# A mask moved from VectorE into TensorE's score sums, and a norm's squares moved to ScalarE, in a two-block transformer kernel

## The reference, cut to what matters

```
z = q . k * 64 ** -0.5
before = s < t
log_1m = where(before, log_sigmoid(-z), 0)
log_rem = reverse_cumsum(log_1m) - log_1m
a = where(before, exp(log_sigmoid(z) + log_rem), 0)
o = a @ v
```

```
a = p[:, :, 0] - lam_full * p[:, :, 1]
o = a @ v
o = rms_norm(o, subln_g) * (1.0 - lam_init)
```

## Time and profile before

| | |
|---|---|
| median of 3 runs | 3639.57 us (3628.84 to 3641.31) |
| span of the profiled execution, first to last instruction | 3623.5 us |
| the profiled execution's own time | not listed apart from the runs |
| TensorE, VectorE, ScalarE busy | 84%, 67%, 35% of the span |
| stick attention | 2152.7 to 2216.1 us |
| differential attention | 2732.4 to 2769.8 us |
| its norm and transposes | 2770.0 to 2785.0 us |
| mean granted clock of TensorE | 0.895 of 2.4 GHz |

### The profile page before, as it was taken

The page is one execution under the profiler, slowest core; times in us unless marked ns, Lnnn a source line. Parts: engine busy times, 40 slices in busy tenths (PEclk is TensorE's granted clock), DMA queues, the critical chain, the costliest instruction groups (busy, mean ns, idle before and its releaser), DMA issues. The chain is left out here.

```text
span 3623.5 us, 52173 instructions
## 1 busy us (share of the span) xinstructions
PE 3031.8 (84%) x21162; PEld 2543.3 (70%) x21162; DVE 2419.6 (67%) x4307; ACT 1260.3 (35%) x2037; POOL 516.0 (14%) x305
## 2 busy tenths in 40 slices
PE   7977765665556699888999988999997999997899
PEld 4856752222211399878989886998986898987798
DVE  3677748888898777555768726777735775556554
ACT  1043211111111234364343445344344434344633
POOL 1010025555455200000000050000041000000000
PEclk9987777777777899979999997999997999998999
DMA  8932228999999786414848531867651774553153
GB/s 340 384 138 95 84 88 364 394 398 395 386 409 404 309 353 232 170 46 188 329 187 351 206 141 47 350 226 308 266 193 61 281 276 171 184 188 113 51 196 126
DMA packets 123103, 854.18 MB, mean 236 GB/s; under 512 B 17301, under 2 KB 18581, under 8 KB 21013
## 3 DMA queue, kind: packets, MB, share of 16 engines
q1 hardware_dynamic: 85748, 582.69, 42.0%
q0 software_dynamic: 36864, 268.45, 18.2%
q10 hardware_dynamic: 288, 0.26, 0.0%
HBM read 850.24 MB, written 1.11 MB: 235 GB/s over the span
## 5 line engine op out<-in xcount | busy, mean ns | idle before, releaser
L193 DVE TENSOR_TENSOR w_lo<-w_ring,w_hi 128x2048 fp32r<-128x2048 f32 x300 | 686.4, 2290 | 508.1 <-ACT w_hi L188 506.2
L268 PE MATMUL ps<-h_hi,w_hi 128*128 128x256 f32 x3328 | 954.9, 287 | 49.8 <-DVE h_lo L459 26.2
L269 PE MATMUL ps<-h_lo,w_hi 128*128 128x256 f32 x3328 | 950.9, 286 | 0.0
L270 PE MATMUL ps<-h_hi,w_lo 128*128 128x256 f32 x3328 | 950.4, 286 | 0.0
L188 ACT ACTIVATE w_hi<-w_ring 128x2048 fp32r<-128x2048 f32 x330 | 629.7, 1913 | 654.7 <-PE ps L270 634.9
L268 PEld LDWEIGHTS ps<-h_hi,w_hi 128*128 128x128 f32 x3328 | 643.8, 193 | 59.6 <-DVE h_lo L459 29.0
L269 PEld LDWEIGHTS ps<-h_lo,w_hi 128*128 128x128 f32 x3328 | 644.0, 194 | 3.2
L270 PEld LDWEIGHTS ps<-h_hi,w_lo 128*128 128x128 f32 x3328 | 643.7, 193 | 0.0
L2955 PE MATMUL ps<-expert_rows,expert_diag 128*128 128x512 f32 x412 | 289.3, 843 | 228.0 <-ACT expert_diag L2996 228.0
L193 POOL TENSOR_TENSOR w_lo<-w_ring,w_hi 128x2048 fp32r<-128x2048 f32 x30 | 138.2, 4622 | 2251.7 <-ACT w_hi L188 2251.7
L2955 PEld LDWEIGHTS ps<-expert_rows,expert_diag 128*128 128x128 f32 x412 | 92.6, 247 | 416.9 <-ACT expert_diag L2996 339.8
(11 more groups left out here) (461 smaller groups left out, 4215.7 us busy)
## 6 DMA issues: line engine op xcount, KB each, us to landing
w_ring<-in_w_stream SPq DMA_DIRECT2D x376, 1024.0 KB, 4.8
a_ring<-in_a_stream SPq DMA_DIRECT2D x108, 1024.0 KB, 7.2
a_ring<-in_t_stream SPq DMA_DIRECT2D x36, 1024.0 KB, 10.0
a_ring<-in_m_stream SPq DMA_DIRECT2D x8, 1024.0 KB, 7.1
alibi<-in_alibi SPq DMA_DIRECT2D x3, 2048.0 KB, 9.0
cond_row<-in_cond_row SPq DMA_DIRECT2D x8, 512.0 KB, 3.8
expert_rows<-in_experts,expert_idx POOLq DMA_INDIRECT x206, 11.8
gates<-mod_rows SPq DMA_DIRECT2D x3, 1024.0 KB, 5.8
```

Source lines behind the costliest of these rows:

```text
L193: pool.tensor_tensor(self.w_halves(n)[1], self.w_item(n), self.w_halves(n)[0], ALU.subtract).then_inc(self.lo_made, 1)
L268: pe.matmul(out, stationary[0], moving[0], start=start, stop=False)
L269: pe.matmul(out, stationary[0], moving[1], start=False, stop=False)
L270: return pe.matmul(out, stationary[1], moving[0], start=False, stop=stop)
```

## The change

The table `before` and its product are dropped. `after` is added by TensorE: for each half one matmul of the identity with `after` is accumulated onto the scores' diagonal block, so that everything made from S sees the mask. The wait for the table stands in front of TensorE's first scores in place of VectorE's first logits. Differential attention takes all heads of token tile 0 first and those of tile 1 after them. ScalarE squares each output from PSUM, with the sum over a head's 128 values, in front of its copy. The norm block then has a scale, a root, a reciprocal and one multiply by tile left; the gain is a column of 128 that the last copies on ScalarE use as their scale, since the transposes have put the head's values on partitions; the transposes go by token tile and wait for their own tile alone. A load of the root's table is asked for at the head of ScalarE's queue in that block.

```diff
@@ attention, vector
-            if mixer.tables:
+            if mixer.tables and not mixer.masked_scores:
                 dve.wait_ge(tables.sem, tables.at(16 * mixer.tables))
@@ Diff
+        self.ss = core.sb(ctx, "diff_ss", [P, TT, DIFF_HEADS])
+        self.sq = core.sb(ctx, "sq", [P, TT, D])
+    def at(self, p):
+        t, h = divmod(p, DIFF_HEADS)
+        return h, t, slice(t * P, (t + 1) * P), causal(t)
     def out(self, act, p):
         h, t, _, _ = self.at(p)
+        act.activation(self.sq[:, t, h * P:(h + 1) * P], self.out_bank(p), ACT.Square, accum_out=self.ss[:, t, h:h + 1])
         return act.activation(self.o[:, t, h * P:(h + 1) * P], self.out_bank(p), ACT.Copy)
@@ Stick
-    tables = 2
+    masked_scores = True
+    tables = 1
     def score(self, pe, p):
         pair, _, tok, n = self.at(p)
-        return [pe.matmul(self.bank(p, half)[:, 0:n], self.qT[part, pair, tok], self.kT[part, pair, 0:n],
-                          start=True, stop=True) for half, part in enumerate(HALVES)]
+        if p == 0:
+            loaded = self.core.semaphore_of("tables_in")
+            pe.wait_ge(loaded.sem, loaded.at(16 * self.tables))
+        for half, part in enumerate(HALVES):
+            pe.matmul(self.bank(p, half)[:, 0:n], self.qT[part, pair, tok], self.kT[part, pair, 0:n],
+                      start=True, stop=False)
+        return [pe.matmul(self.bank(p, half)[:, tok], self.core.ident[:], self.after[:], start=False, stop=True)
+                for half in range(2)]
     def logits(self, dve, p, L, mx):
-        steps.done(dve, dve.tensor_tensor(soft[:, :, tok], soft[:, :, tok], spread(self.before[:], 2), ALU.mult))
...
-        last = dve.tensor_tensor(L[:, :, 0:n], S, scan, ALU.subtract)
-        steps.done(dve, last)
-        return dve.tensor_tensor(L[:, :, tok], L[:, :, tok], spread(self.after[:], 2), ALU.add)
+        return dve.tensor_tensor(L[:, :, 0:n], S, scan, ALU.subtract)
@@ stick_stage
-        projections(core, 12, units, tables=[(n.before[:], "before"), (n.after[:], "after")], led=LEAD)
+        projections(core, 12, units, tables=[(n.after[:], "after")], led=LEAD)
@@ diff_stage
-        g = core.sb(ctx, "subln_g", [P, P])
+        g = core.sb(ctx, "subln_g", [P, 1])
-                            (g[:], core.io["subln_g"].partition_broadcast(P), consts)])
+                            (g[:], core.io["subln_g"], consts)])
@@ its vector
-                core.dve_steps.done(dve, dve.tensor_tensor(sq[:], n.o[:], n.o[:], ALU.mult))
-                core.dve_steps.done(dve, dve.tensor_reduce(st[:, 0], sq4, AX.X, ALU.add))
-                dve.tensor_scalar(st[:, 0], st[:, 0], 1.0 / P, EPS, ALU.mult, ALU.add).then_inc(ss.sem, 1)
+                dve.tensor_scalar(n.ss[:], n.ss[:], 1.0 / P, EPS, ALU.mult, ALU.add).then_inc(ss.sem, 1)
+                dve.tensor_scalar(g[:], g[:], n.keep, None, ALU.mult).then_inc(gained.sem, 1)
                 dve.wait_ge(roots.sem, roots.at(1))
-                core.dve_steps.done(dve, dve.reciprocal(st[:, 1], st[:, 0]))
+                core.dve_steps.done(dve, dve.reciprocal(n.ss[:], n.ss[:]))
                 for t in range(TT):
-                    core.dve_steps.done(dve, dve.tensor_tensor(sq4[:, t], o4[:, t], wide(st[:, 1, t, :], P), ALU.mult))
-                    gb = bass.AP(g[:].tensor, g[:].offset, [list(g[:].ap[0]), [0, DIFF_HEADS], list(g[:].ap[1])])
-                    core.dve_steps.done(dve, dve.scalar_tensor_tensor(
-                        out=sq4[:, t], in0=sq4[:, t], scalar=n.keep, in1=gb, op0=ALU.mult, op1=ALU.mult))
-                    dve.sem_inc(normed.sem, 1)
+                    dve.tensor_tensor(sq4[:, t], o4[:, t], wide(n.ss[:, t, :], P), ALU.mult).then_inc(normed.sem, 1)
@@ its scalar
+                act.preload_act_table_set("sqrt_and_others")
                 act.wait_ge(ss.sem, ss.at(1))
-                act.activation(st[:, 0], st[:, 0], ACT.Sqrt).then_inc(roots.sem, 1)
+                act.activation(n.ss[:], n.ss[:], ACT.Sqrt).then_inc(roots.sem, 1)
+                act.wait_ge(gained.sem, gained.at(1))
                 for k in range(0, KD, 2):
                     act.wait_ge(turned.sem, turned.at(k // 2 + 1))
                     act.activation(oT[:, k:k + 2, :], core.ps[:, k // 2, :].rearrange("p (k n) -> p k n", k=2),
-                                   ACT.Copy)
+                                   ACT.Copy, scale=g[:, 0:1])
@@ its tensor
-                pe.wait_ge(normed.sem, normed.at(TT))
-                for k in range(KD):
-                    for t in range(TT):
+                for t in range(TT):
+                    pe.wait_ge(normed.sem, normed.at(t + 1))
+                    for k in range(KD):
                         last = pe.transpose(core.ps[:, k // 2, (k % 2) * T + t * P:(k % 2) * T + (t + 1) * P],
                                             sq[:, t, k * P:(k + 1) * P], core.ident[:])
-                    if k % 2:
-                        last.then_inc(turned.sem, 1)
+                        if t == TT - 1 and k % 2:
+                            last.then_inc(turned.sem, 1)
```

More of the change, by code:

```diff
@@ L1179 @@
     weighs = True
+    masked_scores = False
     tables = 0
@@ L1449, in __init__ @@
         self.scan = core.sb(ctx, "scan", [P, 2, T])
-        self.before = core.sb(ctx, "before", [P, P])
         self.after = core.sb(ctx, "after", [P, P])
@@ L1472, in logits @@
         core = self.core
-        _, t, tok, n = self.at(p)
+        _, _, _, n = self.at(p)
         soft, scan = self.soft[:, p % 2, :, 0:n], self.scan[:, :, 0:n]
@@ L1676, in diff_stage @@
     normed, turned = core.semaphore_of("diff_normed"), core.semaphore_of("diff_turned")
+    gained = core.semaphore_of("diff_gained")
     with ExitStack() as ctx:
@@ L1690, in diff_stage @@
         with ExitStack() as inner:
[L1691 to L1692 removed]
+            sq = n.sq
             block = inner.enter_context(nc.Block())
@@ L1717, in _ @@
                     act.activation(oT[:, k:k + 2, :], core.ps[:, k // 2, :].rearrange("p (k n) -> p k n", k=2),
-                                   ACT.Copy)
+                                   ACT.Copy, scale=g[:, 0:1])
             @block.tensor
             def _(pe):
-                pe.wait_ge(normed.sem, normed.at(TT))
-                for k in range(KD):
-                    for t in range(TT):
+                for t in range(TT):
+                    pe.wait_ge(normed.sem, normed.at(t + 1))
+                    for k in range(KD):
                         last = pe.transpose(core.ps[:, k // 2, (k % 2) * T + t * P:(k % 2) * T + (t + 1) * P],
                                             sq[:, t, k * P:(k + 1) * P], core.ident[:])
-                    if k % 2:
-                        last.then_inc(turned.sem, 1)
+                        if t == TT - 1 and k % 2:
+                            last.then_inc(turned.sem, 1)
         out_projection(core, oT, 1, 1, 2, tail_room(core.alibi, n.kT))
-    for s in (ss, roots):
+    for s in (ss, roots, gained):
         s.passed(1)
@@ L1813, in attention_tables @@
             cmp_bias[:, h, t] = np.where(near >= 0, -slope * near, np.float32(NEG))
-    before = (np.arange(P)[None, :] < q).astype(np.float32)
-    after = np.where(before > 0, np.float32(0.0), np.float32(NEG))
-    return {"alibi": alibi, "cmp_bias": cmp_bias, "cmp_valid": cmp_valid, "before": before, "after": after,
+    after = np.where(np.arange(P)[None, :] < q, np.float32(0.0), np.float32(NEG))
+    return {"alibi": alibi, "cmp_bias": cmp_bias, "cmp_valid": cmp_valid, "after": after,
             "ident": np.eye(P, dtype=np.float32)}
@@ L1859, in second_layout @@
         "diff_lam": np.ascontiguousarray(a["diff_lam_2"]),
-        "subln_g": np.ascontiguousarray(a["diff_subln_g_2"]),
+        "subln_g": np.ascontiguousarray(a["diff_subln_g_2"].reshape(P, 1)),
     }
```

## The result

| | before | changed |
|---|---|---|
| median | 3636.16 us (6 runs, 3628.84 to 3643.47) | 3617.00 us (6 runs, 3607.18 to 3628.68) |
| profiled execution: its own time, span | not listed, 3623.5 us | 3618.78, 3617.0 us |
| mean granted clock | 0.895 | 0.900 |

A forecast was written before the change was run, and what follows sets the result against it. Stick attention was bound by a three-engine loop, differential attention by TensorE at the low clock, the norm by a plain chain. Terms -5.0 - 0.3 - 7.3 = -12.6 us; 3639.6 - 12.6 = 3627 us, range 3614 to 3637.

The forecast's parts named there:

- turns of the clock: Stick attention: TensorE's clock would take both levels in turn, between -0.4 and -8.0 us, put at -5.0 us.
- six tenths at the high level: Stick attention: gain set six tenths of the way from the low-clock to the high-clock case, giving -5.0 us.
- mask's price: Stick attention: two mask matmuls add at most 2 x 0.43 = 0.86 us to the loop at the low clock.
- 6.9 us of work: Stick attention, low clock: TensorE's 5.2 us of a pair plus 1.72 us of mask matmuls, nearly filling a 7.00 us pair.
- signs for the score groups: Stick attention: score groups for 256 keys would take 2.1 us at clock 0.50 and 1.1 us at 1.00.
- bare one: Differential attention: the last square on ScalarE is not covered by idle time and costs +0.4 us.
- The order: Differential attention: small tiles first, +1.7 us at a low clock, -1.9 us if it rises; taken as -0.7 us.
- the first tile's transposes run under the second: Norm: transposes of the first tile overlap the second 1.26 us multiply, leaving eight; part of the -7.3 us.
- rival 1: Clock stays low in stick attention, mask matmuls replace the saving: 3632 us, 3634 at the worst; chance 0.20.
- rival 2: Clock rises within the first pairs and stays: -16.8 us, 3623 us; chance 0.19.
- rival 3: Square needs another table set than Exp, loads at each tile: +28 to +41 us, 3655 to 3668 us; chance 0.03.
- rival 4: Change does nothing that can be told, gains given back elsewhere: 3638 us; chance 0.06.

The follow-up runs named there:

- four other profiles: Unaltered changed stick attention in the changed kernel again, alone, with squares in the old order and with the root's table early: stages 60.14, 60.31, 61.22 and 60.54 us.
- stick alone: Kernel before with only stick attention changed: median 3618.13 us, ratio 0.9975 (0.9948 to 1.0001), stick stage 60.31 us.
- mask twice: Changed kernel with the mask added twice, four mask matmuls a tile in place of two: stick stage 63.77 us, pairs of 6.66 us at the high clock.
- early table: Changed kernel with the load of the root's table moved from the norm block into differential attention: norm 7.52 us, attention 35.16 us, one run of 3614.33 us.
- second profile: Changed kernel unaltered, measured again beside the kernel before: median 3610.97 us (12 runs), ratio 0.9953 (0.9935 to 0.9972), stick stage 60.14 us.
- float32r mask: Changed kernel with mask table and identity copied to the type float32r: stick stage 60.48 us, seven pairs of 6.71 us.
- filler: Changed kernel with one unused float32r matmul of 512 columns more per stick attention tile: stick stage 57.50 us, one run of 3618.17 us.

## Why the prediction was right, point by point

**Stick attention, -5.0 forecast, -4.5 measured, -2.1 to -3.2 in the four other profiles of it.** VectorE's loss of 0.91 us from the loop is 3.70 - 2.78 = 0.92. The turns of the clock came as forecast, but six tenths at the high level was a choice between two levels that no row gave; the first profile has 0.60, the five together 0.42 to 0.60, so it was the upper end. The mask's price was too small. At the low clock the way from scores to `soft` grew by 4.47 - 3.35 = 1.12 us where I had 0.86; at the high clock it is 3.43 us, and the forecast 3.35 - 1.23 + 0.70 + 0.44 = 3.26. So pairs of 7.25 and 6.21 us instead of 7.00 and 6.05. The term of the sum that was mis-sized is this 0.86 us: I had taken the two matmuls as a continuation of their group, when a group of their own takes 1.15 us (2165.00 to 2166.15) and 0.64 us (2184.90 to 2185.54). It also makes TensorE itself the bound of some low pairs: my 6.9 us of work with 2 x 0.29 more is 7.5, and pairs of 7.5 us are there in several profiles, stick alone among them. My text named this as what could make it wrong, "if the mask's matmuls cost more than 0.43 us each at the low clock". With 1.12 us for two they do; that a further matmul is no dearer than its price is measured at the high clock alone (mask twice, 0.22 us). The signs for the score groups, 2.1 and 1.1 us, were missed by the same: they take 2166.15 - 2163.84 = 2.31 and 2185.54 - 2184.27 = 1.27 us.

The Trainium skill ("TensorE: Matmul & The Clock Gate", Part 1) would have the slow clock released by activity. The trace agrees that it is released here, and shows that it does not stay: within 50 us of this stage the mean is 0.84, with 0.50 from 2178 to 2181 between two stretches at 1.00.

**Differential attention, -0.3 forecast, -1.4 measured.** The squares were +0.4 for the bare one and cost +0.37, but of that the bare one is 2768.61 - 2768.35 = 0.26; the rest came while tiles were running, where VectorE waits for ScalarE twice (0.16 us at 2756.55 and 0.28 at 2764.29), so +0.4 is right in part by luck. The order was -0.7 and is -1.76. Two terms of it were too dear: small tiles run 1.59 to 1.67 us apart and not 1.78, which I had read from a small tile that stood between large ones; and of the large tiles ahead of the rise I had two at 2.74, but the seam between small and large has TensorE at 2.10 us a tile. The rise itself came after four large scores, near 2754, 20 us behind the start of `lam_s`; before, it came near 2761, 27 us behind it. The -0.7 was also two thirds of the way between a case without the rise and one with it, and the rise came.

**Norm, -7.3 forecast, -6.9 measured, in all profiles with it but those with the early table.** The chain is the one that I wrote down: load, root, reciprocal, two multiplies, eight transposes, four copies. The first multiply starts 2770.98 - 2769.15 = 1.83 us behind the start of the table load (forecast 1.86), and the two end at 2773.34. The step that failed, by 0.7 us, is "the first tile's transposes run under the second": they start at 2772.26 and, at 0.21 us each (the granted clock is 0.50), eight of them need 1.7 us where a multiply needs 1.2. So the second tile's transposes start at 2774.02 (the ninth record of the group of 16) and not at 2773.34, and its first bank and copy (2774.76) are late by as much. The copies, 2.42 us for four, were within their bounds. The last one ends at 2777.18, so 8.03 us behind the start of the table load; the forecast was 7.5 to 7.9. 

**Projections, 0 forecast:** +0.8 and -0.2 us here, +0.1 and -0.2 in the second profile. The +0.8 does not repeat. The -0.2 is in seven of the eleven profiles with the new norm (22.65 to 22.74 us), the other four have 22.88 to 24.08; I did not follow it up.

**The rivals.** The clock staying low (rival 1) didn't come in any of the five profiles with the float32 mask, but it is just what the float32r mask has, 0.50 throughout. Rising and staying (rival 2) came from the third pair on in the profile with the filler, 57.50 us. The table load at each square (rival 3) is absent. "Nothing that can be told" (rival 4) is excluded by two intervals that end at 0.9965 and 0.9972.

**Median against stages.** The stages lose 12.2 and 11.6 us in two profiles; the medians lost 19 and 15, with intervals that begin at 12.7 and 10. Ahead of the second measurement I had put 0.9966 (the stages are all) against 0.9945 (7 us more lie elsewhere). It gave 0.9953, and its interval, 0.9935 to 0.9972, leaves both. What lies outside the changed stages scatters by more than that: stick attention starts between 2137.30 and 2157.09 us in the 14 profiles. So whether a few microseconds are won elsewhere is open. The prediction gave 0.71 to a time within 0.5% of the kernel before and 0.25 to a gain above that; the two measurements, 0.54% and 0.47%, lie on either side of that border.

**How much was luck.** The mechanism of each stage is the one forecast, and the sum of the stages, -12.2, is near -12.6 because its errors run against each other: the stick won less (-4.5 in the best profile, -3.1 on average, for -5.0), the norm a little less (-6.9 for -7.3), differential attention more (-1.4 for -0.3). With the average of the stick the sum is -11.4.

## What to carry to other kernels

Price extra matmuls as a group: take the interval from the start of such a group to the start of the next in a trace at each clock, with the same kind of work in front of it and behind it; here the same two matmuls took 1.15, 1.01 or 0.99 us at the low clock by what stood next to them. An edit that moves work onto TensorE can lose at constant clock (7.25 against 7.05 us a pair) and still win when the clock rises with it. Read the granted clock in every pair before crediting the edit, take more than one profile where the clock goes up and down (58.88 to 61.22 us here), and try the kernel without the moved work to see what it really gives back. Where tiles of two sizes alternate through engines with queues of different lead, sort them by size, and cost the seam separately.

## What the runs showed that I had not expected

- A mask group (two float32 matmuls, 128x128 by 128 columns) between scores and values takes 1.15 us at the low clock and 0.64 at the high one, which is 0.29 and 0.20 us above 2 x 0.43 and 2 x 0.22. In front of the scores it takes the same after a wait, and 0.99 and 0.54 us directly behind transposes; with transposes behind it, 1.01 us. Doubling the matmuls adds 0.22 us each at the high clock. What the part that is left is made of was not separated.
- In float32r such a group takes 0.62 us at the low clock, more than half of 1.15.
- TensorE busy for 39.82 of 42 us stayed at a granted clock of 0.50 with the float32r mask; busy for 6.19 of 9 us, it was at 1.00 with the float32 one. The busy time in the rows does not by itself tell the clock; what does is open here.
- A matmul that computes nothing, 0.40 us in each tile's idle time, stood in the shortest stage of all with the float32 mask, 57.50 us against 58.88 to 61.22 (one profile).
- The activation right behind a table load starts 0.02 us after the load's end (2769.15 + 1.28 to 2770.45), and 16 squares among the exponentials needed no load.
